# Layer 0's conditioning product as unsplit float32 strips on TensorE

## The reference, cut to what matters

```python
cond = jax.nn.silu(c)
for i in range(DEPTH):
    mod = cond @ ada_w[i] + ada_b[i]                # (1, 1024) @ (1024, 6144)
    sh1, sc1, g1, sh2, sc2, g2 = jnp.split(mod, 6, axis=-1)
    hm = modulate(x, norm_gain[i, 0], sh1, sc1)     # rms_norm * (1 + scale) + shift
    ...                                             # mix = attention or Mamba-2
    x = x + g1[:, None, :] * mix
    hf = modulate(x, norm_gain[i, 1], sh2, sc2)
    ...                                             # ffn = SwiGLU or experts
    x = x + g2[:, None, :] * ffn
```

## Time and profile before

| | |
|---|---|
| median of 3 runs | 1764.47 us (1763.08 to 1766.15) |
| profiled execution, from first to last instruction | 1763.7 us |
| mean granted TensorE clock in it | 0.978 |
| TensorE busy | 1675.2 us (95%) |
| VectorE busy | 1447.0 us (82%) |
| ScalarE busy | 1116.1 us (63%) |
| DMA, mean | 282 GB/s |
| conditioning of layer 0 with "ada" split | about 15 to 41 us |
| attention of layer 0 | about 97 to 181.5 us |

### The profile page before, as it was taken

How to read it: one execution, slowest core, us unless ns; L and a number is a source line. 1 busy time by engine, 2 the same in 40 slices (tenths; PEclk the granted TensorE clock), 3 DMA queues, 4 the chain that set the end, 5 groups by cost and what they waited for, 6 DMA issues and landing times.

```text
span 1763.7 us, 25287 instructions
## 1 busy us (share of the span) xinstructions
PE 1675.2 (95%) x7621; PEld 1328.8 (75%) x7621; DVE 1447.0 (82%) x1631; ACT 1116.1 (63%) x1357; POOL 0.2 (0%) x4
## 2 busy tenths in 40 slices
PE   7966999999998989899999999999999999999996
PEld 5632677777687777588888888888888888888884
DVE  5578687777547777599899899898998998998995
ACT  6343343443345584378778778777777787787773
POOL 0000000000000000000000000000000000000000
PEclk9987999999999998999999999999999999999998
DMA  8656498878354504189999999999999999999991
GB/s 341 215 177 220 136 371 284 283 273 282 109 204 131 191 1 142 49 303 365 334 371 369 343 356 375 334 366 344 379 353 334 384 357 337 367 367 335 365 374 73
DMA packets 206248, 497.94 MB, mean 282 GB/s; under 512 B 18188, under 2 KB 20541, under 8 KB 206025
## 3 DMA queue, kind: packets, MB, share of 16 engines
q1 hardware_dynamic: 206152, 496.91, 78.8%
HBM read 495.78 MB, written 1.07 MB: 282 GB/s over the span
## 4 chain that ended last, share of the span: by engine, by line
PE 84%; DVE 6%; issue 3%; ACT 2%; DVEq 0%; ACTq 0%
PE acc L1560 25%; PE acc L1567 24%; PE acc L1561 24%; PE xb L1839 2%; PE xb L1805 2%; PE acc L1545 1%; PE xb L1597 1%; DVE cv L1327 1%; PE acc L1933 1%; PE xb L1642 1%; PE acc L1663 1%; DVE w_lo L931 1%; PE xb L1828 1%; PE acc L1655 1%; DVE ada L958 1%
## 5 line engine op out<-in xcount | busy, mean ns | idle before, releaser
L931 DVE TENSOR_TENSOR w_lo<-raw,w_hi 128x1024 fp32r<-128x1024 f32 x848 | 1013.0, 1223 | 171.3 <-ACT w_hi L570 146.0
L570 ACT ACTIVATE w_hi<-raw 128x1024 fp32r<-128x1024 f32 x848 | 882.2, 1059 | 298.4 <-PE acc L1567 288.3
L1560 PE MATMUL acc<-w_hi,g_hi 128*128 128x512 f32 x896 | 354.3, 395 | 1.1 <-DVE g_lo L1506 1.1
L1561 PE MATMUL acc<-w_hi,g_lo 128*128 128x512 f32 x896 | 349.0, 390 | 0.0
L1567 PE MATMUL acc<-w_lo,g_hi 128*128 128x512 f32 x896 | 276.5, 390 | 0.1
L1567 PEld LDWEIGHTS acc<-w_lo,g_hi 128*128 128x128 f32 x896 | 168.1, 188 | 36.2 <-DVE w_lo L931 0.5
L1560 PEld LDWEIGHTS acc<-w_hi,g_hi 128*128 128x128 f32 x896 | 168.3, 188 | 34.6 <-issue 1.2
L1561 PEld LDWEIGHTS acc<-w_hi,g_lo 128*128 128x128 f32 x896 | 168.4, 188 | 33.2
L1560 PE MATMUL acc<-w_hi,a_hi 128*128 128x512 f32 x464 | 185.7, 400 | 6.0 <-DVE a_lo L981 4.5
L1561 PE MATMUL acc<-w_hi,a_lo 128*128 128x512 f32 x464 | 181.8, 392 | 0.0
L1560 PE MATMUL acc<-w_hi,e_hi 128*128 128x512 f32 x448 | 177.9, 397 | 0.0
(11 more groups left out here) (256 smaller groups left out, 1496.4 us busy)
## 6 DMA issues: line engine op xcount, KB each, us to landing
raw<-in_moe_w_gu SPq DMA_DIRECT2D x448, 512.0 KB, 6.0
raw<-in_moe_w_down SPq DMA_DIRECT2D x224, 512.0 KB, 5.3
raw<-in_ada_w SPq DMA_DIRECT2D x96, 512.0 KB, 5.5
raw<-in_ffn_w_gu SPq DMA_DIRECT2D x56, 512.0 KB, 5.5
raw<-in_ssm_w_in SPq DMA_DIRECT2D x40, 512.0 KB, 4.4
raw<-in_ffn_w_down SPq DMA_DIRECT2D x28, 512.0 KB, 5.0
raw<-in_ssm_w_out SPq DMA_DIRECT2D x16, 512.0 KB, 4.3
raw<-in_attn_w_qkv SPq DMA_DIRECT2D x12, 512.0 KB, 13.8
```

Of the source, the lines that this page charges most:

```text
L570: act.activation(w_hi[:, w % SPLIT, :], raw[:, no % RAW, :], ACT.Copy).then_inc(hi_ready, 1)
L931: dve.tensor_tensor(w_lo[:, w % SPLIT, :], raw[:, no % RAW, :], r32(w_hi[:, w % SPLIT, :]), ALU.subtract).then_inc(raw_used, 1)
L1560: pe.matmul(o, l_hi[:, k, rows_], hi[:, col:col + HALF], start=new, stop=False)
L1561: pe.matmul(o, l_lo[:, k, rows_], hi[:, col:col + HALF], start=False, stop=False)
```

## The change

Nothing of layer 0's conditioning is split any more, and VectorE no longer multiplies and adds. For each raw tile (index k of its row) TensorE takes the raw float32 tile as the moving operand, in two halves, and `cond[:, k]` broadcast to 32 columns as the weights. The result goes to one of four strips of 32 output partitions of one PSUM bank: partitions 0 and 32 for the halves of even k, 64 and 96 for those of odd k. The bias row goes first, as two 32-column matmuls (`strips_open`). When a row's 8 tiles are in, VectorE copies the bank to `strips` (in `mod`'s spare slot), and TensorE adds the strips 0 and 64, or 32 and 96, onto all 128 partitions with a weight matrix that has ones at two rows (`sum_of`, made out of `ident`). Both those matmuls are full float32. The raw tile is freed by TensorE through `ada_used` in place of `raw_used`; the counts of `raw_used` are corrected (`lo_count`) everywhere.

The diff, cut (`lo_count` and `is_strip` only choose which counter a load waits for; the other edits of `raw_used` waits put the corrected number; `ada_beside` goes from five places of `unit_scores` and `unit_probs`, `ada_bias`, `ada_sum` and `ada_tiles` go whole):

```diff
@@ sync: load @@
-                if no >= RAW:
-                    sp.wait_ge(raw_used, no - RAW + 1 + rep(e, BODY))
+                if no >= RAW and is_strip(no - RAW):
+                    sp.wait_ge(ada_used, no - RAW + 1 - lo_count(no - RAW))
+                elif no >= RAW:
+                    sp.wait_ge(raw_used, lo_count(no - RAW) + rep(e, BODY))
@@ scalar @@
-            act.wait_ge(cond_ready, 1)
-            act.activation(cond_hi[:, :], cond[:, :], ACT.Copy).then_inc(cond_ready, 1)
...
-            ada_hi(0, 2 * KD)
             early_hi("qkv")
             norm(0, "norm0")
@@ vector @@
-            dve.tensor_tensor(cond_lo[:, :], cond[:, :], r32(cond_hi[:, :]), ALU.subtract).then_inc(cond_ready, 1)
+            dve.wait_ge(ld_square, 32)
+            for hf in range(2):
+                dve.tensor_tensor(sum_of[:, hf:hf + 1], ident[:, 32 * hf:32 * hf + 1], ident[:, 64 + 32 * hf:65 + 32 * hf],
+                                  ALU.add).then_inc(sum_ready, 1)
+            def strips_in(c):
+                dve.wait_ge(ada_used, (c + 1) * KD)
+                if c:
+                    dve.wait_ge(ada_ready, c)
+                dve.tensor_copy(strips, acc[ada_pair(c) % 3][:, 0:HALF]).then_inc(strips_out, 1)
             def ada_row(c):
...
+                dve.wait_ge(ada_ready, c + 1)
...
             norm_root(0)
-            for i in range(2 * KD):
-                split_lo(raw0["ada"] + i, spl0["ada"] + i)
-                if i == KD + 1:
-                    ada_row(0)
+            strips_in(0)
+            ada_row(0)
             early_lo("qkv")
+            strips_in(1)
             ada_row(1)
             ada_rows_stand(0, 1)
             norm(0, "norm0")
...
-                ada_beside(beside, 0)
...
             for u in range(8):
                 if u < 7:
...
-                    unit_scores(u + 1, u)
-                else:
-                    ada_beside(u, 0, 1, 2)
+                    unit_scores(u + 1)
+                if u and u % 2 == 0:
+                    ada_row(1 + u // 2)
                 unit_probs(u)
                 if u:
                     heads_lo(u - 1)
-                ada_beside(u, 5, 6, 7)
-                if u >= 3 and u % 2:
-                    ada_row((u + 1) // 2)
+                if u % 2:
+                    strips_in(2 + u // 2)
             early_lo("wo")
             heads_lo(7)
+            ada_row(5)
             gemm("wo", (KD,))
-            ada_row(5)
@@ tensor @@
-            ada_tiles()
+            def strip(c, k):
+                no = (raw0["ada"] if c < 2 else raw0["attend"] - 2 * KD) + c * KD + k
+                pe.wait_ge(raw_ready[no % RAW], 16 * (no // RAW + 1))
+                o = acc[ada_pair(c) % 3]
+                for hf, cols in enumerate(HALVES):
+                    j = 32 * (2 * (k % 2) + hf)
+                    mm = pe.matmul(o[j:j + 32, 0:HALF], cond[:, k:k + 1].to_broadcast([P, 32]), raw[:, no % RAW, cols],
+                                   start=k == 1, stop=k >= KD - 2, skip_group_check=True)
+                mm.then_inc(ada_used, 1)
+            def strips_open(c):
+                pair = ada_pair(c)
+                open_pair(pair % 3, pair // 3)
+                for hf, cols in enumerate(HALVES):
+                    pe.matmul(acc[pair % 3][32 * hf:32 * hf + 32, 0:HALF], ident[0:12, c:c + 1].to_broadcast([12, 32]),
+                              bias_rows[:, cols], start=True, stop=False, skip_group_check=True)
+            def strip_pair(c, k):
+                if k == 0:
+                    strips_open(c)
+                strip(c, k)
+                strip(c, k + 1)
+            def strips_sum(c):
+                if c == 0:
+                    pe.wait_ge(sum_ready, 2)
+                pe.wait_ge(strips_out, c + 1)
+                o = acc[ada_pair(c) % 3]
+                for hf, cols in enumerate(HALVES):
+                    mm = pe.matmul(o[:, cols], sum_of[:, hf:hf + 1].to_broadcast([P, P]), strips, start=True, stop=True)
+                mm.then_inc(ada_ready, 1)
+            for c in range(2):
+                for k in range(0, KD, 2):
+                    strip_pair(c, k)
+                    if c == 1 and k == 0:
+                        strips_sum(0)
+            strips_sum(1)
             norm(0, "norm0", pr0["qkv"])
...
             for u in range(8):
+                if u and u % 2 == 0:
+                    strips_sum(1 + u // 2)
                 if u:
                     attend(u - 1)
                 if u < 6:
                     scores(u + 2)
+                for k in range(0, PER_UNIT, 2):
+                    strip_pair(2 + u // 2, PER_UNIT * (u % 2) + k)
                 turn_probs(u)
                 if u < KV - 1:
                     bias_turn(u + 1)
-                if u and u % 2 == 0:
-                    ada_sum(1 + u // 2)
             attend(7)
-            ada_sum(5)
+            strips_sum(5)
```

More of the change, by code:

```diff
@@ L114, in build @@
     cond = place("cond", [P, KD])
-    cond_hi, cond_lo = (place(n, [P, KD], f32r) for n in ("cond_hi", "cond_lo"))
+    sum_of = place("sum_of", [P, 2])
     ss, ms, rs = (place(n, [P, 2]) for n in ("ss", "ms", "rs"))
@@ L141, in build @@
     reversal = mod[:, 6, 0:P]
+    strips = mod[:, 6, HALF:2 * HALF]
     q_t = place("q_t", [P, KD, SEQ], f32, U_AT + 28672)
@@ L235, in build @@
         sem(n) for n in ("relb_set", "cond_ready", "ada_ready", "ld_gain"))
+    ada_used, strips_out, sum_ready = (sem(n) for n in ("ada_used", "strips_out", "sum_ready"))
     ss_ready, ms_ready, root_ready, hm_ready, x_ready = (
@@ L270, in build @@
     for stage, raws, splits, pieces, pairs in (
-        ("start", 0, 0, 2, 0), ("ada", 2 * KD, 2 * KD, 0, 2), ("norm0", 0, 0, 4, 0),
+        ("start", 0, 0, 2, 0), ("ada", 2 * KD, 0, 0, 2), ("norm0", 0, 0, 4, 0),
         ("qkv", 12, 12, 0, 4), ("heads", 0, 0, 6 + 2, 0), ("attend", 4 * KD, 0, 20 + 6, 12),
@@ L280, in build, with lo_count, is_strip @@
         at = [a + b for a, b in zip(at, (raws, splits, pieces, pairs))]
+    def lo_count(no):
+        early = min(max(no + 1 - raw0["ada"], 0), 2 * KD) + min(max(no + 1 - raw0["attend"], 0), 4 * KD)
+        return no + 1 - early
+    def is_strip(no):
+        return raw0["ada"] <= no < raw0["ada"] + 2 * KD or raw0["attend"] <= no < raw0["attend"] + 4 * KD
     def body_pieces(mixture):
@@ L641, in _ @@
             norm_root(0)
-            def ada_hi(first, n):
-                for i in range(first, first + n):
-                    split_hi(raw0["ada"] + i, spl0["ada"] + i)
-            ada_hi(0, 2 * KD)
             early_hi("qkv")
@@ L954, in ada_half @@
                     if hf:
-                        dve.wait_ge(raw_used, no)
+                        dve.wait_ge(raw_used, lo_count(no - 1))
                     else:
@@ L1117, in _, with unit_scores @@
                                       qk_gain[:, 1:2, :].to_broadcast([P, KV, HD]), ALU.mult).then_inc(qk_ready, 1)
[L1119 to L1126, removed]
+            def unit_scores(u):
                 g, blk = UNITS[u]
@@ L1145, in unit_scores @@
                 done = step(dve.reduce_max(stat[:, u % 2, 0, :], s3, axis=AX.X))
-                ada_beside(beside, 1)
                 dve.wait_ge(dve_step, done)
                 done = step(dve.tensor_tensor(top_, top_, sink, ALU.max))
-                ada_beside(beside, 2)
                 dve.wait_ge(dve_step, done)
@@ L1178, in heads_lo @@
                                   ALU.subtract).then_inc(xb_done[c % 2], 1)
-            unit_scores(0, -1)
+            unit_scores(0)
             for u in range(8):
@@ L1224, in body @@
                         if k == 0 and c >= 2:
-                            dve.wait_ge(ada_ready, 4 + c - 1)
+                            dve.wait_ge(ada_ready, 6 + c - 1)
                         for hf in range(2):
@@ L1562, in weight_tile @@
                     if t == 0:
-                        pe.wait_ge(raw_used, no + 1 + rep(e, BODY))
+                        pe.wait_ge(raw_used, lo_count(no) + rep(e, BODY))
                     for m, (k, to, col) in enumerate(parts):
@@ L1648, in _ @@
             HALVES = (slice(0, HALF), slice(HALF, 2 * HALF))
-            def ada_bias(c):
+            def strip(c, k):
[7 more added lines that the diff above has]
+                mm.then_inc(ada_used, 1)
@@ L1652, in ada_bias @@
+            def strips_open(c):
                 pair = ada_pair(c)
                 open_pair(pair % 3, pair // 3)
[L1654 to L1663, removed]
-                mm.then_inc(ada_ready, 1)
@@ L1666, in ada_tiles @@
[L1666 to L1682, removed]
@@ L1686, in _ @@
+            pe.wait_ge(cond_ready, 1)
+            for c in range(2):
[4 more added lines that the diff above has]
+            strips_sum(1)
             norm(0, "norm0", pr0["qkv"])
@@ L1847, in _ @@
                     if n % KD == 0:
-                        ada_group_end[n // KD - 1] = Body(False).raw_no(s) + 2
```

(1 more changed line is left out.)

9 lines of the change are left out of this document (removed).

## The result

The changed kernel takes 1748.13 us (median of 4 runs, 1746.23 to 1751.31), the one before 1765.31 in the same comparison. The ratio is 0.9903 (95% interval 0.9891 to 0.9915). It is faster by 17.2 us, 1.0%; forecast were 10.7. The profiled execution spans 1745.7 us, 18.0 less than the 1763.7 of before.

The account below looks back on a forecast made before the run. VectorE was taken to bound attention, TensorE nearly everywhere else. The span 1763.7 - 17.7 (attention) + 7.0 (start) = 1753.0, with 0.8 for the median 1753.8, was called 1754 us; range 1747 to 1768.

Parts of the forecast that it names:

- The bound: Attention: VectorE bounds it, 44.1 us of multiply-adds on the path, transposes waiting 26.0 us, nearly all for `sc`.
- The price of a strip: Conditioning matmuls: four strips of 32 run at once, so a unit's four tiles take 1.9 us at full clock.
- the estimate of 3.17 times for four: Strips: speed-up taken from the skill page's 2.38 for three; a unit 0.45 us dearer, 3 us over seven.
- Part 1, the start: Before `norm(0)`: `strips_sum(1)` waits for VectorE's copy behind the qkv splits, clock falls; a loss of 7 us.
- Part 2, attention: Attention to "wo": units 1 to 7 sum to 48.4 us, "wo" starts 17.7 us earlier.
- VectorE's chain is shorter in each: Attention units: VectorE's chain takes 4.6 us in odd and 6.7 in even units, less than TensorE's pieces.
- To this I add 3.5 us: Attention's beginning: added to the 48.4 us for the low clock, with unit 1's pieces partly at it.
- The clock low in attention: Rival, attention: clock stays low, 33 us more if throughout; total 1767 at 52% low, 1783 at all; chance 0.17.
- Two at once: Rival, attention's strips: only two run together, 12 us more, total 1766; chance 0.13 shared with exposed loads.
- one after another: Rival, attention's strips: no overlap, 6.9 us a unit for 1.72, 36 us more, total 1790; chance 0.07.
- exposed loads: Rival, attention's strips: 16 uncovered weight loads a unit, 5 to 21 us, total 1759 to 1775; chance 0.13 shared.
- No loss at the start: Rival, the start: qkv tile split sooner, TensorE never waits, total 1747; chance 0.08.

Follow-up runs that it names:

- e3: Changed kernel, but attention's strips use only output partitions 0 and 32, for even and odd k alike; 1762.89 us, ratio 0.9989 to the kernel before.
- e4: Changed kernel, but all of attention's strip matmuls go to output partitions 0 to 31, halves in two banks; 1800.88 us.
- e1: Changed kernel, with VectorE's copy of row 1's strips moved ahead of the three early qkv splits; 1742.49 us, ratio 0.9873 to the kernel before.
- e2a: Changed kernel's start only (rows 0 and 1 by strips), attention keeps VectorE's multiply-adds; 1769.74 us, ratio 1.0029 to the kernel before.
- e2b: Changed kernel's attention only (rows 2 to 5 by strips), the start keeps its splits; 1745.5 us, ratio 0.9895 to the kernel before.
- e6: e1 plus the first two "wo" splits ahead of attention's last copies, third and fourth around the last heads' parts; 1737.46 us, ratio 0.9844 to the kernel before.
- e7: e2b with 12 in place of 9 keep_warm matmuls before the first norm; 1745.68 us, ratio 0.9891 to the kernel before.
- e5: Changed kernel, but each strip matmul in attention has 16 columns in place of 512, leaving out nearly all of rows 2 to 5; 1744.88 us.

## Why the prediction was right, and what it missed

*The bound.* Right: VectorE bound attention, and its multiply-adds were on the path; the transposes' wait for `sc` went from 25.7 to 2.7 us.

*The price of a strip.* Right: four tiles took 1.92 us at full clock, forecast 1.9. e3 and e4 show by themselves that four run at once and that two or one cost 3.63 or 7.05. Weight loads are not exposed: a unit has 16 of 32 columns, 0.108 us each, 1.7 us in all, and its matmuls take 1.92 us with them, which is 4 times 0.43 and the latency. The Trainium skill ("TensorE: Matmul & The Clock Gate", Part 3) has 2.38 times for three strips; the estimate of 3.17 times for four, worked out from that, would have made 2.2 us, 2.4 with the latency. The trace doesn't agree: 1.92 us, 3.7 times faster than e4's 7.05. Nor does it agree with the same part of the Trainium skill where it says that loads overlap running matmuls only where the row group differs.

*Part 1, the start.* Right in mechanism, place and size: 7 forecast, 6.4 measured. `strips_sum(1)` began at 43.35 (forecast 43.75), after the forecast idleness, at the forecast low clock; `keep_warm` ended at 55.6 (56.4), since the clock rose at 48.6, not 50. e1 shows that the order on VectorE is the cause. e2a shows that it goes through to the end: 5.4 us by the medians, of 5.8 at `scores(0)`. In the changed kernel e1 gets 5.6 of it back.

*Part 2, attention.* The sum over units 1 to 7 was forecast at 48.4 us and measured at 48.3 (transposes' ends from 110.95 to 159.29). Unit by unit: 7.7, 9.1, 6.3, 7.9, 5.3, 7.9, 4.2, for the forecast 6.8, 9.2, 6.8, 7.9, 5.5, 7.9, 4.3; unit 1 took 0.9 us more, unit 3 0.5 less, and units 2, 5 and 7 0.1 or 0.2 less, so that the sum came out to 0.1 us partly by luck. In unit 1 "VectorE's chain is shorter in each" was wrong: VectorE waited 3.7 us for the bias from ScalarE, and TensorE 1.0 us for `sc`. From the last transposes to "wo" 6.7, forecast 6.8. The moved `ada_row(5)` cost nothing.

*The step that was mis-sized* is the last term of that sum, "To this I add 3.5 us, since the stretch begins at the low clock", with the first transposes "at low clock". It measured 0. The low stretch from 101 us on the earlier trace rows came with TensorE's gap of 6.6 us before the first transposes of probabilities. The strips of unit 0 now fill that gap to 1.73 us, and the clock stayed up there in the changed kernel, e1, e2b, e6 and e7. In e2a, with the gap of before (6.58), it fell; in e5, whose short strips leave 3.34 us, it fell too, and `bias_turn` took 3.56 us for 1.98. These transposes before, in the changed kernel, and in e5:

```profile
105.86 1.11 PE L1597 MATMUL xb<-square,sc 128*128 128x128 f32 x4 [6.57 <-DVE sc L1168]
110.29 0.66 PE L1592 MATMUL xb<-square,sc 128*128 128x128 f32 x4 [1.73 <-DVE sc L1164]
110.10 1.12 PE L1592 MATMUL xb<-square,sc 128*128 128x128 f32 x4 [3.34 <-DVE sc L1164]
```

I carried a clock state over that the change itself removes. With 0.6 for the transposes (their end at 104.5 without the start's 6.4, forecast 105.1) and 0.1 for other pieces this makes 4.2 us, the start's 0.6 come to it, and 2.5 came after "wo", which the sum put at nothing. Together 7.3, the difference of -10.7 and -18.0. By the medians, -17.2, the time lies 1 us above the lower end of the stated range, 1747, which was put there for just this case, a full clock from the first unit, though with a start only 4 us late. The 2.5 are explained only in part: 0.6 is the first "wo" matmuls, which ran at the low clock before and don't now; 1.2 lies within the "proj" product of layer 1, where each kernel has a low stretch of 3.4 us, but at another tile. No run looked into that, and by the spread given in the result such an amount comes and goes between traces of the same instructions.

*The rivals.* The clock low in attention: not in the changed kernel, but real, as e2b (0.91) and e7 (0.97) show; with e2b's low stretch the change would have gained 4.5 us less. That the traced execution had none is in part luck. Two at once, one after another, exposed loads: refuted by e3, e4 and the rows. No loss at the start: refuted, and made by e1.

## What to carry to other kernels

When an engine's queue gets a wait on a result that another engine makes, look at what stands ahead of that result in the other engine's order: moving one copy ahead of three splits was worth 5.6 us. A vector by matrix product in float32 costs TensorE about a quarter (1.92 us for 7.05) when it is laid on four strips of 32 output partitions, and then it is worth moving off a VectorE that is the bound. When work moves onto TensorE into its gaps, price it at the clock it will then have, not at the one that went with the gaps. Before a difference of a few us between two traces is explained by an edit, look whether the same instructions take the same time in both, ahead of the edit and behind it: here they differed by up to 2.2 us ahead and 4.6 behind.

## What the runs showed of the hardware

- Float32 matmuls of 128 rows, 32 output partitions and 512 columns: 16 records take 1.92 us on four strips, 3.63 on two (e3), 7.05 on one (e4), though they stand one behind the other in one queue; in e4 the matmuls of the one strip went to two banks and didn't overlap.
- Float32 adding matmuls 32 rows deep took as long as ones 128 deep (1.12 and 1.02 us for one in e4, 1.98 for two in the changed kernel).
- In e2b a granted clock of 0.5 for some 10 us followed a gap of TensorE of 1.54 us; in the traces of four other kernels the same gap was followed by none (changed kernel, e6) or about 3.4 us of it (e1, e7). 4.5 us, 0.26% of the kernel, hang on that. Whether the place in time decides it or the single execution is open.
- The same instructions from the second norm to the end took 1556.6 to 1561.0 us in ten traces.
- With a single strip at work the mean clock was 0.94 although TensorE was busy for 91% of the stretch (e4).
